# Rebuilding the beginning of a two-block kernel: raw tokens turned once, inverse roots spread by a product, half tiles normed on GpSimd

## The chip, the cores and the metric

The kernel runs on one core of a Trainium2 chip. The metric is the device time of one execution in microseconds (us); several executions are taken and their median is given. The engines are named as the profile names them: PE (TensorE; PEld its weight loads), DVE (VectorE), ACT (ScalarE), POOL (GpSimd) and SP (SyncE, which issues the DMAs).

## The reference

Two transformer blocks over 512 tokens of 1024 channels, in float32. Only the entry of the first block matters here: 16 meta tokens are put ahead of the 512, every row is normed (times the inverse root of its mean square plus 1e-6, times a weight per channel), and the result is multiplied by `w_in`.

```python
h = jnp.concatenate([meta, x], axis=1)      # 16 + 512 tokens, then padding
n = _rms(h, norm_mix_w[l])                  # x * rsqrt(mean(x*x) + eps) * w
z = n @ w_in[l]                             # 1024 -> 9216 channels
q, k, v, glu, g_att, g_conv = jnp.split(z, splits, axis=-1)
...
h = h + m @ w_out[l]                        # the raw h is needed again
```

Attention, a gated convolution, a feed-forward block and a whole second block follow, which the change does not touch.

## The kernel before, in words

Activations are held channel-major: `hT` has 128 channels of a tile on the partitions, 8 tiles (k) and 528 token columns (16 meta + 512). A float32 product is made of three fp32r products: weights and activations are split into a high part and the rest (`wh`, `wl`; `xh`, `xl`), and wh x xh, wh x xl and wl x xh are summed in PSUM. Weights come in chunks of two halves of 128 columns over all 8 k; chunk n uses slot n % 2 of `raw`, `wh` and `wl`. For each chunk ACT makes the high part (`hi(n)`, L1415), DVE the low part (`lo(n)`, L1969), and PE multiplies each half in 8 x 3 x 2 matmuls of 264 columns (`project`, L679).

The order on every engine is written out by hand; each engine runs its own list in order, and semaphores tie the lists together. The beginning before the change:

- SP loads the norm weight row, the meta tokens, four token tiles of 128 tokens each (`xrow`, L537), chunk 0 of the weights in three pieces (k 0-1, 2-3, 4-7, L541), chunk 1, and then some thirty small constants.
- ACT squares each token tile with a row sum (L1442) and takes its root (L1443). DVE inverts the root and scales the tile by it, token-major, into `xn` (L1994).
- PE turns each raw tile (`raw_tokens`, L773, eight transposes of 128x128) for `hT`, and DVE or ACT copies it there (`keep_tokens`, L1998). Separately PE turns the normed tiles, one k at a time over all four token tiles (`normed_tokens`, L780). ACT makes `xh` of that, weighted per channel (L1451), and DVE `xl` (L2007), both from PSUM. The 16 meta columns go through `mn` and `mw` on a path of their own.
- Chunk 0 is multiplied k by k over both token halves (L810), with the transposes of k + 3 behind each k. Then PE turns raw tiles 2 and 3, waits for their copy, and goes on with chunk 1 (`project(ALLP[2], 1, 0, ...)`), whose first half stands ahead of some transposes of constants, and with all later chunks.
- ACT makes the high part of chunk 1 after its token high parts, and DVE `lo(1)` after its token low parts.
- POOL sets constants at the start (L610 to L616) and later copies small attention pieces (L623, L628).

Of the kernel before, what the change touches and what calls it, by code (L numbers as in the profile page):

```python
# [16 lines left out]
D = 1024  # L17
KT = D // 128
# [84 lines left out]
def program(nc, A, out):  # L103
# [17 lines left out]
    with ExitStack() as ctx:  # L121
# [58 lines left out]
        mw = at("mw", [128, KT, NM])  # L180
        xn = at("xn", [128, TT, D])
        mn = at("mn", [NM, D])
# [121 lines left out]
        s_xn = sem("tokens_normed")  # L304
        s_mt = sem("meta_transposed")
        s_mx = sem("meta_weighted")
        s_ms = sem("meta_split")
        s_nt = sem("normed_tokens_transposed")
# [167 lines left out]
        def _(sp):  # L476
# [57 lines left out]
            sp.dma_start(wrow[:], A["norm_mix_w"][0].rearrange("(g p) -> g p", p=128)).then_inc(s_wm, 16)  # L534
            sp.dma_start(mrow[:], A["meta_tokens"]).then_inc(s_min, 16)
            for t in range(TT):
                sp.dma_start(xrow[:, t, :], x[128 * t:128 * (t + 1), :]).then_inc(s_xin[t], 16)  # L537
            G = 3 * D
            for j, (k, signal) in enumerate(zip(PIECES, (s_r0[0], s_r0[1], s_raw[0]))):
# [69 lines left out]
        def _(pool):  # L609
# [6 lines left out]
            pool.memset(eps5[:], 1e-5).then_inc(s_id, 1)  # L616

# [33 lines left out]
        def _(pe):  # L651
# [124 lines left out]
            def normed_tokens(k):  # L776
                if k >= 3:
                    pe.wait_ge(s_nl, k - 2)
                for t in range(TT):
                    ins = tr(scores_ps[:, k % 3, 128 * t:128 * (t + 1)], xn[:, t, 128 * k:128 * (k + 1)], ident[:])  # L780
                ins.then_inc(s_nt, 1)

            pe.wait_ge(s_wm, 16)
            tr(scores_ps[:, 3, 0:8], wrow[:], ident[0:8, 0:8]).then_inc(s_wt, 1)
            pe.wait_ge(s_xin[0], 16)
            raw_tokens(0, psP[0])
            pe.wait_ge(s_min, 16)
            pe.wait_ge(s_xn, 1)
            for k in range(KT):
                tr(scores_ps[:, 3, 128 + NM * k:128 + NM * (k + 1)], mn[:, 128 * k:128 * (k + 1)], ident[0:NM, 0:NM])  # L790
                ins = tr(scores_ps[:, 3, 256 + NM * k:256 + NM * (k + 1)], mrow[:, 128 * k:128 * (k + 1)], ident[0:NM, 0:NM])
            ins.then_inc(s_mt, 1)
            pe.wait_ge(s_xin[1], 16)
            raw_tokens(1, psP[1])
            pe.wait_ge(s_xn, TT + 1)
            for k in range(3):
                normed_tokens(k)
            pe.wait_ge(s_hm, 2)
            pe.wait_ge(s_ms, 2)
            pe.wait_ge(s_l0, 1)  # L800
            for k in range(KT):
                if k == PIECES[1].start:
                    pe.wait_ge(s_l0, 2)
                if k == PIECES[2].start:
                    pe.wait_ge(s_lo, 1)
                pe.wait_ge(s_nl, k + 1)
                for half in range(2):
                    for p, (W, Y) in enumerate(((wh, xh), (wh, xl), (wl, xh))):
                        for a in range(2):
                            ins = mm(psP[half][:, a, 0:HT], W[:, 0, half, k, :], Y[:, k, a * HT:(a + 1) * HT],  # L810
                                     start=(k == 0 and p == 0), stop=(k == KT - 1 and p == 2))
                    if k == KT - 1:
                        ins.then_inc(s_mm, 1)
                if k + 3 < KT:
                    normed_tokens(k + 3)
            for t in range(2, TT):
                pe.wait_ge(s_xin[t], 16)
                raw_tokens(t, psS[t - 2])
# [584 lines left out]
        def _(act):  # L1403
# [31 lines left out]
            act.wait_ge(s_wt, 1)  # L1435
            fn(vmix[:], scores_ps[:, 3, 0:8], ACT.Copy).then_inc(s_wc, 1)
# [3 lines left out]
            for t in range(TT):  # L1440
                act.wait_ge(s_xin[t], 16)
                own(fn(flat, xrow[:, t, :], ACT.Square, accum_out=rcol[:, t:t + 1]))  # L1442
                fn(rcol[:, t:t + 1], rcol[:, t:t + 1], ACT.Sqrt, bias=eps6[:], scale=1.0 / D).then_inc(s_rs, 1)  # L1443
# [5 lines left out]
            def normed_hi(k):  # L1449
                act.wait_ge(s_nt, k + 1)  # L1450
                fn(xh[:, k, NM:T], scores_ps[:, k % 3, :], ACT.Copy, scale=vmix[:, k:k + 1]).then_inc(s_nh, 1)  # L1451

            act.wait_ge(s_mx, 1)
            fn(xh[:, :, 0:NM], mw[:], ACT.Copy).then_inc(s_ms, 1)
            first_hi(0)
            act.wait_ge(s_xt, 2)
            fn(hT[:, :, NM + 128:NM + 256], psP[1][:].rearrange("p a (b c) -> p (a b) c", c=128), ACT.Copy).then_inc(s_hm, 1)
            normed_hi(0)
            normed_hi(1)
            first_hi(1)  # L1460
            normed_hi(2)
            first_hi(2)
            for k in range(3, KT):
                normed_hi(k)
# [497 lines left out]
        def _(dve):  # L1962
# [48 lines left out]
            for t in range(TT):  # L2011
                norm_tokens(t + 1, 128, xrow[:, t, :], xn[:, t, :])
                if t == 0:
                    keep_tokens(0, psP[0])
# [701 lines left out]
```

## Time and profile before

| what | value |
|---|---|
| median of 3 runs | 1545.5 us (1545.24 to 1545.65) |
| the profiled execution | 1544.58 us, span of its instructions 1542.8 us |
| PE busy | 1526.5 us (99%) |
| DVE busy | 1119.0 us (73%) |
| ACT busy | 645.7 us (42%) |
| POOL busy | 29.6 us (2%) |

The profiled execution is a single one, so its time stands beside its span: 1.8 us lie outside of the span. Busy shares are means over the whole span and say little of its first 40 us, which the change touches. Times in the views count from the start of the span.

### The profile page before, as it was taken

What the parts mean: (1) busy time and instruction counts of PE and PEld (TensorE: products, weight loads), DVE (VectorE), ACT (ScalarE), POOL (GpSimd) and SP (SyncE); (2) the same over time, 40 slices, a digit from 0 to 9 for tenths busy, and PEclk for the clock granted to TensorE, in tenths of its full rate; (3) what the DMA queues carried; (4) which work ended last, traced back from release to release, by engine and by line L of the source; (5) the groups of instructions that cost most, each with busy time, mean ns of one, the idle gap of its engine ahead of it and who ended that gap; (6) DMA issues with size and microseconds to landing.
All of it is one profiled execution on the core that took longest, in us unless ns stands there. A gap on an engine that the chain in (4) does not pass through costs nothing.

```text
span 1542.8 us, 25468 instructions
## 1 busy us (share of the span) xinstructions
PE 1526.5 (99%) x9972; PEld 1364.0 (88%) x9972; DVE 1119.0 (73%) x1662; ACT 645.7 (42%) x1014; POOL 29.6 (2%) x66
## 2 busy tenths in 40 slices
PE   8999999999999999999999999999999999999998
PEld 7999999999999999999988888878888888888887
DVE  5889998989665587777764458987748888787123
ACT  5324545545542434434424335744545333333112
POOL 0000010000000000000000020000000000000000
PEclk9999999999999999999999999999999999999999
DMA  6333222232233333233232443231131333332221
GB/s 179 83 92 100 56 69 70 56 83 56 56 89 103 83 101 90 82 103 87 65 94 78 117 110 83 55 82 42 55 110 56 107 92 101 83 107 96 109 82 55
DMA packets 235358, 131.63 MB, mean 85 GB/s; under 512 B 20984, under 2 KB 228740, under 8 KB 235284
## 3 DMA queue, kind: packets, MB, share of 16 engines
q1 hardware_dynamic: 234900, 130.40, 30.1%
q8 instruction: 52, 0.85, 0.2%
q0 software_dynamic: 384, 0.20, 0.1%
q14 instruction: 22, 0.18, 0.0%
HBM read 128.48 MB, written 2.10 MB: 85 GB/s over the span
## 4 chain that ended last, share of the span: by engine, by line
PE 91%; DVE 5%; ACT 3%; issue 1%; DMA 0%; SPq 0%; DVEq 0%; ACTq 0%
PE psP L679 31%; PE psS L679 25%; PE psP L744 8%; PE psS L1363 4%; PE psP L1363 4%; PE psP L701 4%; PE psP L1054 3%; PE psP L1231 1%; DVE conv L2080 1%; PE psS L1231 1%; PE psP L901 1%; DVE wl L1969 1%; PE psS L858 1%; PE psP L810 1%; PE psS L1120 1%
## 5 line engine op out<-in xcount | busy, mean ns | idle before, releaser
L1969 DVE TENSOR_TENSOR wl<-raw,wh 128x2048 fp32r<-128x2048 f32 x124 | 284.0, 2290 | 178.0 <-ACT wh L1415 176.6
L1415 ACT ACTIVATE wh<-raw 128x2048 fp32r<-128x2048 f32 x124 | 237.0, 1912 | 210.0 <-PE psS L1363 74.3
L679 PE MATMUL psP<-xh,wh 128*128 128x258 f32 (+2 forms) x1184 | 295.6, 312 | 1.6 <-ACT mqk L1745 0.6
L679 PE MATMUL psP<-xh,wl 128*128 128x258 f32 (+2 forms) x1184 | 291.6, 309 | 0.0
L679 PE MATMUL psP<-xl,wh 128*128 128x258 f32 (+2 forms) x1184 | 291.4, 309 | 0.0
L679 PE MATMUL psS<-xh,wh 128*128 128x258 f32 (+2 forms) x880 | 209.9, 305 | 0.4 <-DVE hT L1998 0.4
L679 PE MATMUL psS<-xh,wl 128*128 128x258 f32 (+2 forms) x880 | 208.5, 304 | 0.0
L679 PE MATMUL psS<-xl,wh 128*128 128x258 f32 (+2 forms) x880 | 208.1, 303 | 0.0
L679 PEld LDWEIGHTS psP<-xh,wh 128*128 128x128 f32 x1184 | 192.8, 190 | 16.2 <-issue 2.4
L679 PEld LDWEIGHTS psP<-xl,wh 128*128 128x128 f32 x1184 | 192.6, 189 | 12.0 <-issue 0.2
L679 PEld LDWEIGHTS psP<-xh,wl 128*128 128x128 f32 x1184 | 192.4, 189 | 11.9
L2080 DVE SCALAR_TENSOR_TENSOR conv<-u,cdw,conv 128x516 f32<-128x516 f32 x232 | 160.4, 749 | 3.1 <-ACT conv L1483 2.4
L679 PEld LDWEIGHTS psS<-xh,wh 128*128 128x128 f32 x880 | 141.9, 189 | 8.0 <-DVE hT L1998 0.7
L679 PEld LDWEIGHTS psS<-xl,wh 128*128 128x128 f32 x880 | 141.7, 189 | 7.1
L679 PEld LDWEIGHTS psS<-xh,wl 128*128 128x128 f32 x880 | 141.5, 189 | 7.0
L1655 ACT ACTIVATE acth<-prod 128x512 f32 x44 | 27.7, 629 | 196.4 <-DVE prod L2299 196.4
L2293 DVE SCALAR_TENSOR_TENSOR acc<-upr,fdw,acc 128x512 f32<-128x512 f32 x88 | 66.1, 752 | 12.2 <-DVE acc L2292 6.4
L2294 DVE SCALAR_TENSOR_TENSOR acc<-upr,fdw,acc 128x512 f32<-128x512 f32 x88 | 66.2, 752 | 12.1 <-DVE acc L2293 6.4
L744 PE MATMUL psP<-actl,wh 128*128 128x512 f32 x176 | 69.6, 396 | 0.0
L744 PE MATMUL psP<-acth,wl 128*128 128x512 f32 x176 | 69.6, 395 | 0.0
L744 PE MATMUL psP<-acth,wh 128*128 128x512 f32 x176 | 69.6, 395 | 0.0
L2292 DVE TENSOR_SCALAR acc<-upr,fdw 128x512 f32<-128x512 f32 x88 | 48.1, 546 | 17.2 <-DVE upr L2289 16.9
(465 smaller groups left out, 2423.9 us busy)
## 6 DMA issues: line engine op xcount, KB each, us to landing
raw<-in_w_in_dram SPq DMA_DIRECT2D x74, 512.0 KB, 4.9
raw<-in_w_up_dram SPq DMA_DIRECT2D x44, 512.0 KB, 4.9
raw<-in_ffn_up_dram SPq DMA_DIRECT2D x44, 512.0 KB, 5.0
raw<-in_ffn_down_dram SPq DMA_DIRECT2D x22, 512.0 KB, 4.1
raw<-in_w_out_dram SPq DMA_DIRECT2D x16, 512.0 KB, 4.5
raw<-in_w_down_dram SPq DMA_DIRECT2D x16, 384.0 KB, 3.6
raw<-in_w_down_dram SPq DMA_DIRECT2D x16, 320.0 KB, 4.0
raw<-in_w_conv_out_dram SPq DMA_DIRECT2D x8, 512.0 KB, 4.6
```

What stands on the lines that cost most here:

```text
L679: ins = mm(ps[0:rows, a, 0:nn], W[:, s, half, k, 0:rows], Y[:, k, c0 + a * nn:c0 + (a + 1) * nn], start=(k == 0 and p == 0), stop=(k == KT ...
L701: ins = mm(ps[0:r, a, 0:nn], W[:, s, half, k, 0:r], Y[:, k, c0 + a * nn:c0 + (a + 1) * nn], start=(k == 0 and p == 0), stop=(k == KT - 1 a ...
L744: ins = mm(ps[:, 0, :], W[:, k, :], Y[:, kk, :], start=(kk == 0 and p == 0), stop=(kk == FG - 1 and p == 2))
L1054: ins = mm(psP[0][:, half, 256 * a:256 * (a + 1)], Y[:, k, o:o + 128], W[:, n % 2, :, k, :], start=(k == 0 and p == 0), stop=(k == KT - 1 ...
L1231: ins = mm(ZP[t][c], Y[:, k, tok], w, start=(k == 0 and p == 0), stop=(k == KT - 1 and p == 2))
L1363: ins = mm(ALLP[t][:, half, :], Y[:, kk, tok], W[:, j, :], start=(kk == 0 and p == 0), stop=(kk == FG - 1 and p == 2))
L1415: fn(wh[:, n % 2], raw[:, n % 2], ACT.Copy).then_inc(s_hi, 1)
L1969: V.tensor_tensor(wl[:, n % 2], raw[:, n % 2], wh[:, n % 2].bitcast(f32), ALU.subtract).then_inc(s_lo, 1)
L2080: V.scalar_tensor_tensor(y, src, w, y, ALU.mult, ALU.add).then_inc(s_v, 1)
L2292: own(V.tensor_scalar(acc[:, x, :], upr[:, j, x, 4:4 + S], w[2], w[3], ALU.mult, ALU.add))
L2293: own(V.scalar_tensor_tensor(acc[:, x, :], upr[:, j, x, 3:3 + S], w[1], acc[:, x, :], ALU.mult, ALU.add))
L2294: V.scalar_tensor_tensor(acc[:, x, :], upr[:, j, x, 2:2 + S], w[0], acc[:, x, :], ALU.mult, ALU.add).then_inc(s_cva, 1)
```

## The change: what it does

Token-major norming goes. Each raw token tile is turned once, into `hT`. The inverse roots, one per token and token-major, are put on the diagonal of a 128x128 matrix per tile (`diag`), and a product of an all-ones matrix with two such diagonals gives, on all 128 partitions, a row with the inverse roots of 256 tokens. DVE copies it to `rb`. A normed half tile (264 columns of one k) is then `hT` times `rb`: k 0 of the first half is made on DVE, the other fifteen on POOL, into a new `xn`. ACT and DVE make `xh` and `xl` of it, now from SBUF and in half tiles; the meta columns take the same path. PE multiplies chunk 0 by token halves: first all k of columns 0 to 263, then all k of the rest, in the order wh x xh, wl x xh, wh x xl, with the spreading product of the second half behind k 4 of the first. All four raw tiles are turned ahead of chunk 0. Fourteen products of the identity with itself come first on PE. SP loads meta and two token tiles first and mixes weight pieces with the others. The diff, with declarations of semaphores and buffers cut:

```diff
@@ SP @@
+            sp.dma_start(mrow[:], A["meta_tokens"]).then_inc(s_min, 16)
+            tokens(0)
+            tokens(1)
+            sp.dma_start(wrow[:], A["norm_mix_w"][0].rearrange("(g p) -> g p", p=128)).then_inc(s_wm, 16)
+            tokens(2)
+            piece(0, s_r0[0])
+            tokens(3)
+            piece(1, s_r0[1])
+            piece(2, s_raw[0])
             pair(w_in, 1, None, 0, G + 128, G + D + 128)
             inputs()
@@ POOL @@
+            for a in range(2):
+                pool.wait_ge(s_rc, 2 + a)
+                pool.wait_ge(s_hm, 2 * (a + 1))
+                for k in range(1 - a, KT):
+                    if a == 0 and k == 1:
+                        pool.wait_ge(s_xn, 1)
+                    pool.tensor_tensor(xn[:, a, k, :], hT[:, k, a * HT:(a + 1) * HT], rb[:, a * HT:(a + 1) * HT],
+                                       ALU.mult).then_inc(s_xn, 1)
@@ PE @@
-            def normed_tokens(k):
...
+            def spread(t):
+                pe.wait_ge(s_dg, 2 + t // 2)
+                mm(psP[1][:, 1, 128 * t:128 * (t + 2)], ones[:], diag[:, t:t + 2, :].rearrange("p t q -> p (t q)"),
+                   start=True, stop=True).then_inc(s_rb, 1)
+
+            def first_products(a, k):
+                Y = slice(a * HT, (a + 1) * HT)
+                if a == 0 and k == 0:
+                    pe.wait_ge(s_h0, 1)
+                if a == 0 and k == PIECES[1].start:
+                    pe.wait_ge(s_l0, 2)
+                if a == 0 and k == PIECES[2].start:
+                    pe.wait_ge(s_lo, 1)
+                pe.wait_ge((s_fh, s_nh)[a], k + 1)
+                for half in range(2):
+                    mm(psP[half][:, a, 0:HT], wh[:, 0, half, k, :], xh[:, k, Y], start=(k == 0), stop=False)
+                if a == 0 and k == 0:
+                    pe.wait_ge(s_l0, 1)
+                for half in range(2):
+                    mm(psP[half][:, a, 0:HT], wl[:, 0, half, k, :], xh[:, k, Y], start=False, stop=False)
+                pe.wait_ge((s_f0, s_nl)[a], k + 1)
+                for half in range(2):
+                    ins = mm(psP[half][:, a, 0:HT], wh[:, 0, half, k, :], xl[:, k, Y], start=False, stop=(k == KT - 1))
+                    if a == 1 and k == KT - 1:
+                        ins.then_inc(s_mm, 1)
+
+            for _ in range(14):
+                mm(psP[0][:, 0, 0:128], ident[:], ident[:], start=True, stop=True)
+            pe.wait_ge(s_xin[0], 16)
+            raw_tokens(0, psS[0])
...
+            pe.wait_ge(s_xin[1], 16)
+            raw_tokens(1, psS[1])
...
+            pe.wait_ge(s_hm, 1)
+            pe.wait_ge(s_xin[2], 16)
+            raw_tokens(2, psS[0])
+            spread(0)
+            pe.wait_ge(s_hm, 2)
+            pe.wait_ge(s_xin[3], 16)
+            raw_tokens(3, psS[1])
             for k in range(KT):
...
+                first_products(0, k)
+                if k == 4:
+                    spread(2)
             for k in range(KT):
...
+                first_products(1, k)
             pe.wait_ge(s_hm, 3)
             project(ALLP[2], 1, 0, X, 0, HT, None)
@@ ACT @@
+            def token_roots(t):
+                fn(rcol[:, t:t + 2], rcol[:, t:t + 2], ACT.Sqrt, bias=eps6[:], scale=1.0 / D).then_inc(s_rs, 1)
...
+            def normed_hi(a, k):
+                act.wait_ge(s_xn, KT * a + k + 1)
+                fn(xh[:, k, a * HT:(a + 1) * HT], xn[:, a, k, :], ACT.Copy, scale=vmix[:, k:k + 1]).then_inc((s_fh, s_nh)[a], 1)
+
+            token_square(0)
+            token_square(1)
+            token_roots(0)
+            token_square(2)
+            act.wait_ge(s_wt, 1)
+            fn(vmix[:], psP[1][:, 0, 0:8], ACT.Copy).then_inc(s_wc, 1)
             first_hi(0)
+            token_square(3)
+            act.wait_ge(s_wc, 1)
+            normed_hi(0, 0)
+            normed_hi(0, 1)
+            token_roots(2)
             first_hi(1)
+            normed_hi(0, 2)
+            normed_hi(0, 3)
             first_hi(2)
+            for k in range(4, KT):
+                normed_hi(0, k)
+            for k in range(KT):
+                normed_hi(1, k)
@@ DVE @@
+            def diagonals(t):
+                dve.wait_ge(s_rs, 2 + t // 2)
+                own(V.reciprocal(rcol[:, t:t + 2], rcol[:, t:t + 2]))
+                for j in range(t, t + 2):
+                    ins = V.tensor_scalar(diag[:, j, :], ident[:], rcol[:, j:j + 1], None, ALU.mult)
+                ins.then_inc(s_dg, 1)
+
+            def copy_roots(t):
+                dve.wait_ge(s_rb, 2 + t // 2)
+                V.tensor_copy(rb[:, NM + 128 * t:NM + 128 * (t + 2)], psP[1][:, 1, 128 * t:128 * (t + 2)]).then_inc(s_rc, 1)
...
+            def first_normed_lo(a, k):
+                dve.wait_ge((s_fh, s_nh)[a], k + 1)
+                Y = slice(a * HT, (a + 1) * HT)
+                V.scalar_tensor_tensor(xl[:, k, Y], xn[:, a, k, :], vmix[:, k:k + 1], xh[:, k, Y].bitcast(f32),
+                                       ALU.mult, ALU.subtract).then_inc((s_f0, s_nl)[a], 1)
...
+            keep_tokens(1, psS[1])
+            diagonals(0)
+            copy_roots(0)
+            dve.wait_ge(s_hm, 2)
+            dve.wait_ge(s_rc, 2)
+            V.tensor_tensor(xn[:, 0, 0, :], hT[:, 0, 0:HT], rb[:, 0:HT], ALU.mult).then_inc(s_xn, 1)
             first_lo(0)
+            dve.wait_ge(s_wc, 1)
+            first_normed_lo(0, 0)
+            first_normed_lo(0, 1)
+            keep_tokens(2, psS[0])
             first_lo(1)
+            first_normed_lo(0, 2)
+            diagonals(2)
+            first_normed_lo(0, 3)
             first_lo(2)
+            first_normed_lo(0, 4)
+            copy_roots(2)
+            keep_tokens(3, psS[1])
+            for k in range(5, KT):
+                first_normed_lo(0, k)
+            for k in range(KT):
+                first_normed_lo(1, k)
...
             lo(1)
-            for t in range(2, TT):
-                keep_tokens(t, psS[t - 2])
```

## Rows read from the trace of the kernel before

**Rows 1.** The page, chain of work that ended last: share of the span by engine.

```profile
PE 91%; DVE 5%; ACT 3%; issue 1%; DMA 0%; SPq 0%; DVEq 0%; ACTq 0%
```

**Rows 2.** That chain in the first 100 us: start us, us, what, xcount.

```profile
2.53 5.88 DMA xrow<-in_x_dram
...
12.32 2.82 PE psS L780 x12
15.14 1.81 PE psP L810 x12
...
29.39 0.89 PE psS L773 x8
...
30.30 1.24 DVE hT L1998
...
31.57 6.11 PE psS L679 x48
...
44.65 11.68 PE psP L679 x96
```

**Rows 3.** Tile view of `xrow`: duration ns min/median/max, first and last start us.

```profile
L773 PE MATMUL psP<-ident,xrow x16: 421/421/475, 5.4 to 10.7; 128*128 128x128 f32 x16
...
L773 PE MATMUL psS<-ident,xrow x16: 271/272/273, 29.2 to 30.9; 128*128 128x128 f32 x16
```

**Rows 4.** Timeline of the beginning, all engines: start us, us, engine line op.

```profile
0.75 0.41 SPq L534 DMA_DIRECT2D wrow<-in_norm_mix_w_dram  x1
...
5.44 1.97 PE L773 MATMUL psP<-ident,xrow 128*128 128x128 f32 x8 [2.90 <-DMA xrow<-in_x_dram]
...
9.15 1.97 PE L773 MATMUL psP<-ident,xrow 128*128 128x128 f32 x8
...
9.78 0.28 DVE L2019 COPY hT<-psS 128x128 f32<-128x128 f32 x1
...
12.38 0.69 DVE L2003 TENSOR_TENSOR wl<-raw,wh 128x512 fp32r<-128x512 f32 x1
...
17.09 1.23 DVE L2003 TENSOR_TENSOR wl<-raw,wh 128x1024 fp32r<-128x1024 f32 x1
...
25.62 1.91 ACT L1415 ACTIVATE wh<-raw 128x2048 fp32r<-128x2048 f32 x1
...
27.56 2.29 DVE L1969 TENSOR_TENSOR wl<-raw,wh 128x2048 fp32r<-128x2048 f32 x1 [1.05 <-ACT wh L1415]
```

**Rows 5.** Timeline of DVE in the second block, operations of 256 columns.

```profile
1159.19 0.48 DVE L2635 SCALAR_TENSOR_TENSOR xl<-hT,vec,xh 128x256 fp32r<-128x256 f32 x1
1159.59 0.48 DVE L2629 SCALAR_TENSOR_TENSOR hT<-psP,vec,hT 128x256 f32<-128x256 f32 x1
```

**Rows 6.** Groups by line, 1100 to 1250 us: xcount | busy us, mean ns | idle before.

```profile
L1921 ACT ACTIVATE xh<-hT,vec 128x256 fp32r<-128x256 f32 x16 | 8.0, 507 | 2.3 <-DVE hT L2629 2.2
```

**Rows 7.** Timeline of PE: four float32 products with the all-ones matrix.

```profile
411.83 1.03 PE L757 MATMUL psP<-sacc,ones 128*128 128x258 f32 x4
```

**Rows 8.** Timeline of POOL: two copies of attention values, one select.

```profile
163.12 1.93 POOL L623 COPY vr<-qkv 128x64 f32<-128x64 f32 x1 [0.49 <-ACT qkv L1514]
...
194.77 2.17 POOL L623 COPY vr<-qkv 128x64 f32<-128x64 f32 x1
...
915.59 2.66 POOL L635 TENSOR_SCALAR_AFFINE_SELECT sel<-sel 4x512 f32<-4x512 f32 x1
```

**Rows 9.** Timeline of DVE at the same three places.

```profile
162.67 2.29 DVE L1969 TENSOR_TENSOR wl<-raw,wh 128x2048 fp32r<-128x2048 f32 x1 [0.16 <-ACT wh L1415]
...
194.56 2.29 DVE L1969 TENSOR_TENSOR wl<-raw,wh 128x2048 fp32r<-128x2048 f32 x1
...
915.49 2.28 DVE L1969 TENSOR_TENSOR wl<-raw,wh 128x2048 fp32r<-128x2048 f32 x1
```

**Rows 10.** Groups of POOL by line: xcount | busy us, mean ns | idle before.

```profile
L631 POOL MEMSET wab<- 128x768 f32 x1 | 0.7, 739 | 520.1 <-PE psS L757 520.1
...
L638 POOL TENSOR_SCALAR_AFFINE_SELECT tri<-tri 128x128 f32<-128x128 f32 x1 | 0.3, 283 | 0.0
```

More of the change, by code:

```diff
@@ L533, in _, with tokens, piece @@
             x = A["x"][0]
-            sp.dma_start(wrow[:], A["norm_mix_w"][0].rearrange("(g p) -> g p", p=128)).then_inc(s_wm, 16)
-            sp.dma_start(mrow[:], A["meta_tokens"]).then_inc(s_min, 16)
-            for t in range(TT):
+            G = 3 * D
+            def tokens(t):
                 sp.dma_start(xrow[:, t, :], x[128 * t:128 * (t + 1), :]).then_inc(s_xin[t], 16)
-            G = 3 * D
-            for j, (k, signal) in enumerate(zip(PIECES, (s_r0[0], s_r0[1], s_raw[0]))):
+            def piece(j, signal):
+                k = PIECES[j]
                 for half in range(2):
                     sp.dma_start(raw[:, 0, half, k], kp(w_in)[:, k, G + D * half:G + D * half + 128]).then_inc(signal, 16)
+            sp.dma_start(mrow[:], A["meta_tokens"]).then_inc(s_min, 16)
[7 more added lines that the diff above has]
+            piece(2, s_raw[0])
             pair(w_in, 1, None, 0, G + 128, G + D + 128)
@@ L798, in _ @@
-            pe.wait_ge(s_hm, 2)
-            pe.wait_ge(s_ms, 2)
-            pe.wait_ge(s_l0, 1)
-            for k in range(KT):
[L802 to L815, printed above, removed]
@@ new lines, in _ @@
+            for _ in range(14):
+                mm(psP[0][:, 0, 0:128], ident[:], ident[:], start=True, stop=True)
+            pe.wait_ge(s_xin[0], 16)
+            raw_tokens(0, psS[0])
+            pe.wait_ge(s_min, 16)
+            for k in range(KT):
+                ins = tr(psP[0][:, 1, 128 + NM * k:128 + NM * (k + 1)], mrow[:, 128 * k:128 * (k + 1)], ident[0:NM, 0:NM])
+            ins.then_inc(s_mt, 1)
+            pe.wait_ge(s_dg, 1)
+            mm(psP[0][:, 1, 0:NM], ones[0:NM, :], diag[0:NM, TT, 0:NM], start=True, stop=True).then_inc(s_rb, 1)
@@ new lines, in _ @@
+            own(V.reciprocal(rcol[0:NM, TT:TT + 1], rcol[0:NM, TT:TT + 1]))
+            V.tensor_scalar(diag[0:NM, TT, 0:NM], ident[0:NM, 0:NM], rcol[0:NM, TT:TT + 1], None, ALU.mult).then_inc(s_dg, 1)
+            keep_tokens(0, psS[0])
+            dve.wait_ge(s_mt, 1)
+            dve.wait_ge(s_rb, 1)
+            V.tensor_copy(hT[:, :, 0:NM], psP[0][:, 1, 128:128 + KT * NM].rearrange("p (k c) -> p k c", c=NM))
+            V.tensor_copy(rb[:, 0:NM], psP[0][:, 1, 0:NM]).then_inc(s_rc, 1)
+            keep_tokens(1, psS[1])
@@ L2029, in _ @@
+            diagonals(2)
+            first_normed_lo(0, 3)
             first_lo(2)
-            for k in range(3, KT):
-                first_normed_lo(k)
+            first_normed_lo(0, 4)
[3 more added lines that the diff above has]
+                first_normed_lo(0, k)
+            for k in range(KT):
+                first_normed_lo(1, k)
             def constants():
@@ L2044, in _ @@
             lo(1)
-            for t in range(2, TT):
-                keep_tokens(t, psS[t - 2])
+            dve.wait_ge(s_f0, KT)
+            dve.wait_ge(s_nl, KT)
             V.memset(u[:, :, 0:PAD], 0.0)
```

81 lines of the change are left out of this document (12 added, 69 removed).

## The prediction, as it was made before the run

> **What bounds the kernel now.** I read the chain of work that ended last first. TensorE holds 91% of it [rows 1], so the edited beginning matters only by when TensorE's unbroken run starts. The chain inside the first 100 us shows that moment [rows 2]: it passes from token tile 2's landing (2.53 + 5.88 = 8.41) through roots and norms to the normed transposes at 12.32, the first chunk's products at 15.14, the two late raw tiles at 29.39 and the copy at 30.30, and at 31.57 chunk 1's first half begins. From there on TensorE runs without a hole, 11.68 us a chunk. So the question is when that half chunk can begin after the change; call it S, 31.57 now. What follows S is the same instructions in the same order, and I count a shift of S in full at the end.
>
> Next I read the tile view of `xrow` [rows 3]: a transpose takes 421 ns at the start and 272 ns later. I read these as the 1.2 and the 2.4 GHz level: TensorE's clock rises only at about 15 us here. Then the timeline of the beginning, for durations [rows 4].
>
> **The change, first stretch: to the first half tile.** Meta and token loads move ahead of the weight row, whose issue takes 0.41 us; token tile 0, on which TensorE starts at 5.44, should land near 4.95 [rows 4]. Fourteen products on the identity come first, from about 1.7 us; at the lower level eight transposes of the same 128 columns take 1.97 us, so these end by about 4.8 and delay nothing. Then, on TensorE, eight transposes (1.97, ends 6.95), eight small meta transposes instead of sixteen (those filled 7.41 to 9.15, so 0.6 with the clock up, 1 without) and one small product, 0.25, to 7.8. Token tile 1: 1.1 us at the upper level, 1.97 at the lower. I take the upper from here, since TensorE has then worked from 1.7 us on; to 8.95. VectorE copies the tile (1.24, as at 30.30 [rows 2]) to 10.2; a reciprocal and two 128-column diagonals, no row of their shape, lie between nothing and two 128-column copies (0.28 each [rows 4]) and a reciprocal: 0.4, to 10.6. The spreading product has 256 columns: four such with 258 took 1.03 us together [rows 7], so one alone, with start and tail, lies between a quarter of that and the whole; I take 0.48, to 11.1. The copy of 256 columns from PSUM lies between 0.28 (128) and 1.24 (1024), 0.42 on their line; to 11.6. The first product on VectorE, 264 columns, 0.43 on the line through 0.69 (512) and 1.23 (1024) [rows 4]; to 12.06. ScalarE's high part of it, 0.51 [rows 6], to 12.6. First matmul at 12.7, against 15.14: the head gains 2.4 us.
>
> **Second stretch: the first half's queue on VectorE.** The new order puts between that product and the low part of tile (0, 4): three weight low parts (0.60, 0.60, 1.15 without their overlapped tails), a raw tile copy (1.14), root work (0.45) and five low parts of 264 columns. Two such of 256 start 0.39 to 0.40 us apart [rows 5], so 1.98 for five. Sum 5.92, tail 0.08: 6.0 us. At the same time GpSimd makes its seven products. Here the trace has something to say. GpSimd's 64-column copies at 163.12 and 194.77 took 1.93 and 2.17 us and ended at 165.05 and 196.94, each 0.09 us after VectorE's weight low part, which reads two SBUF tensors (162.67 + 2.29 = 164.96; 194.56 + 2.29 = 196.85) [rows 8, 9]. So GpSimd doesn't read beside such an operation. All VectorE's low parts here are of that kind. Whether VectorE is held in turn by a long GpSimd instruction no row shows, since those copies are too short: held not at all is one end, for the whole instruction the other. I take the second, because the first is already exclusive.
>
> What a GpSimd product of two 264-column inputs takes has no row either. The select on 512 columns ended at 918.25, 0.48 us after VectorE's low part (915.49 + 2.28 = 917.77) had let it go [rows 8, 9]; as the copies need less than 0.09 us past such an end, I give it 0.57. The 128-column one took 0.283, and a memset writes 768 columns in 0.739, 0.96 ns each [rows 10]. The line through the two selects gives 0.38 for one input of 264; that is the lower end, a second input free. Doubled, 0.76 is the upper. A second input as one more pass, somewhat under the memset's rate, at 0.83 ns a column, makes 0.38 + 0.22 = 0.60, which I take.
>
> With seven products of 0.60 (4.2 us) beside these 6.0 us, about half falls under the raw copy from PSUM or under VectorE's waits for ScalarE; I charge VectorE 2.1 us. Low part (0, 4) is ready at 12.06 + 6.0 + 2.1 = 20.2.
>
> **Third stretch: what the second half waits for.** The spreading product of the second half stands on TensorE behind the products of tile 4, so behind that low part: 0.3 for the last two matmuls, 0.48 product, 0.42 copy, then raw tile 3's copy, 1.24: 22.6. Only then may GpSimd begin its eight products; it first lets one low part pass, 0.3. One turn is a product and a low part, less the overlaps seen above (0.09 at a GpSimd start; 0.48 lasts, 0.40 apart): 0.60 - 0.09 + 0.48 - 0.08 = 0.91, say 0.88 with ScalarE's time between hidden. Last product at 22.9 + 7 x 0.88 + 0.60 = 29.7. TensorE's six matmuls a tile (0.73 from 0.122 each, 11.68 / 96 [rows 2]) fit under the turn. What is late next is chunk 1's weight: its high part is queued on ScalarE behind all sixteen token high parts, its low part on VectorE behind all sixteen low ones, and chunk 1 waits for it. So 0.46 for the last high part, then 1.91 and 2.29 [rows 4], with 0.1 for hops: S = 34.45. Before, this pair ran at 25.62 and 27.56, ended at 29.85 and cost nothing, covered by the rest of chunk 0; that cover of 1.7 us is gone.
>
> 34.45 - 31.57 = +2.9 us. The removed work (32 normed transposes, 2.82 us for the first twelve, and the two late raw tiles) is in this: TensorE alone could be through chunk 0 at 12.7 + 96 x 0.122 + 0.48 = 24.9, against 29.39, and the elementwise chain gives that back. SP's queue keeps its bytes. Tile 0 and tile 2 landed 3.0 us apart, 1.5 us for 512 KB, so in the new order the weight pieces land near 8.9, 11.1 and 13.0; ScalarE comes to them at 9.3, 13.9 and 15.4 and they cost nothing, each late microsecond of the first would cost one. The constants' loads keep their place and have until S + 6 us. Chunk 2's weight load waits for the third weight low part, 19.8, and stands behind the constants' loads anyway.
>
> On the profiled execution's own 1544.58 us (span 1542.8) this makes 1547.5; the runs' median lies 0.9 above that execution, so 1548.4.
>
> **A rule weighed.** The rows show GpSimd held by VectorE [rows 8, 9]. The Trainium skill (SBUF — State Buffer, section "SBUF: two separate sides") says more: the pair of ports that the two engines share is an exclusive lock, taken for a whole instruction by whichever starts first, and a VectorE operation with two SBUF inputs is locked out by a GpSimd one that reads SBUF. By that rule the sum stands as made; the trace agrees in the one direction that it shows. The Trainium skill (GPSIMD Engine Reference, section "3.1 Elementwise — side-by-side cycle accounting") gives 4497 ns for a two-input product of 2048 columns, by proportion 0.58 us for 264 columns, an estimate; the sum by it would be about 0.3 us lower, and no run here shows it yet.
>
> **The rivals.**
> GpSimd waits but holds nobody, or the two share freely. For: no row shows VectorE held. Against free sharing: GpSimd does wait [rows 8, 9]. Then a turn is 0.60 to 0.75, VectorE's 2.1 us fall away in part or whole, and S comes to between 30.0 (free) and 32.4 (GpSimd alone waits): 1543.9 to 1546.3. With a free second input (0.38) as well, 2.9 us are gained, 1542.6; nothing in the order lets it go further, since the chain of stretches two and three remains.
>
> The GpSimd product costs more than I take: the other side. Place: the eight products of the second half and the seven of the first. Price: 0.1 us more on each adds about 1.45 us, so 0.76 gives +5.2, 1550.7. It decides from about 0.62 us a product, where S is 3.1 us late and the loss passes 0.2%. For it: two-input work on GpSimd has no row. Against it: the select's 0.283.
>
> The clock doesn't come up. The identity products are to raise it before the tokens; if it stays at 1.2 GHz until about 13 us, tile 1 and the spreading product cost 2.0 us more on the path: 1550.4. For: in the trace TensorE worked from 5.44 to 11.1 with small holes and was still at the lower level at 12.32, twelve transposes in 2.82 us [rows 2 to 4]. Against: there are 3 us of extra work ahead now.
>
> **How the numbers follow.** 0.2% of this kernel, 3.1 us, is about what a measurement can tell from no change. My case (both held, product near 0.60, 1547 to 1549.2) gets 0.37, a fifth of it beyond 1548.6; the sharing rival 0.31, nearly all within 0.2%; the costlier product 0.19, the late clock 0.07, both slower; 0.06 is left for something that I don't see and that gains over 3.1 us. So faster 0.06, slower 0.19 + 0.07 + 0.08 and some for the sharing rival with a late clock, 0.37, same 0.57. The range runs from the lower sharing case, 1543.6, to the costlier product just beyond its bound, 1551.5.
>
> **What would show it.** In the changed trace: first matmul of the chunk near 12.7; GpSimd's products longer than 0.7 us where a low part is under way, and low parts longer than 0.48; the second spreading product after 20 us; the eight GpSimd products of the second half from about 23; high and low part of chunk 1's weight after 29.7 and directly ahead of S. It is wrong if S stands below 30, if TensorE alone sets the end of chunk 0, or if GpSimd's products come at steps over 1.1 us.

## The result, and the profile after

The changed kernel takes 1551.4 us (median of 6 runs, 1550.62 to 1553.62) against 1545.4 for the kernel before beside it (1544.76 to 1546.49): ratio 1.0042, 95% interval 1.0032 to 1.0052. It is slower by 0.4%. I had forecast 1548.4, 2.9 us later, and "no change" as likeliest; the loss is about twice that. The time lies just inside the range, and that is luck: the range ended where it did because of the costlier product, which is not what cost the time.

The chain's shares first, the line that answers to [rows 1]. POOL, which had no part in the chain, now has 1% of it:

```profile
PE 90%; DVE 6%; ACT 3%; issue 1%; POOL 1%; DVEq 0%; POOLq 0%; ACTq 0%
```

The chain in the first 100 us (start us, us, what), which answers to [rows 2]:

```profile
1.68 5.42 PE psP L824 x28
...
12.99 0.45 DVE xn L2069
...
21.58 0.81 PE psP L812 x2
22.39 0.44 PE psP L816 x2
22.83 0.44 PE psP L819 x2
23.27 0.87 PE psP L799 x2
...
24.58 1.14 DVE hT L2043
...
25.86 7.19 POOL xn L636 x8
...
33.49 1.91 ACT wh L1446
...
35.43 2.30 DVE wl L2009
...
37.87 6.08 PE psS L700 x48
...
50.91 11.68 PE psP L700 x96
```

Chunk 1 begins at S = 37.87 in place of 31.57, and from there the steps are the old ones: 6.08 us for its first half (before 6.11), 11.68 a chunk. The spans, 1549.1 and 1542.8, differ by the same 6.3 us. So all of the loss lies ahead of S. The chain names it: 28 records of identity products, a stretch at 21.6 in which a pair of matmuls takes 0.44 us, eight POOL products one behind the other, then the weight of chunk 1, high part and low part.

Windows of the changed kernel: start and end, length, busy us (instructions) of PE, PEld, DVE, ACT and POOL, then the granted TensorE clock, DMA share, GB/s.

```profile
13.00:31.50 18.50, 13.73 (x69) 11.79 (x68) 15.82 (x23) 8.37 (x17) 11.94 (x14) 0.72 0.48 122
...
18.00:20.00 2.00, 1.48 (x10) 1.05 (x9) 1.96 (x5) 1.43 (x4) 1.90 (x3) 0.91 0.29 88
20.00:22.00 2.00, 1.23 (x4) 0.92 (x5) 1.93 (x3) 0.45 (x1) 0.00 (x0) 0.50 0.29 72
...
28.00:30.00 2.00, 2.00 (x12) 2.00 (x10) 2.00 (x3) 1.20 (x3) 2.00 (x3) 0.53 0.59 151
30.00:32.00 2.00, 2.00 (x19) 2.00 (x18) 2.00 (x3) 1.03 (x2) 2.00 (x3) 1.00 0.00 0
```

The first of these windows in the kernel before:

```profile
13.00:31.50 18.50, 18.13 (x143) 17.57 (x141) 11.21 (x14) 10.56 (x13) 0.00 (x0) 1.00 0.51 133
```

Before, PE worked 18.1 of these 18.5 us at the upper level. Now it works 13.7, part of it at the lower level (0.50 of full speed, 1.2 GHz, from 19.6 to 29.9), while DVE went from 11.2 to 15.8 us. The limit has moved from PE to DVE and POOL.

The tile views of `xl`, `xn` and `diag` (duration ns min/median/max) show why both are so full:

```profile
L2053 DVE SCALAR_TENSOR_TENSOR xl<-xn,vmix,xh x16: 479/974/993, 14.2 to 33.7; 128x264 fp32r<-128x264 f32 x16
...
L636 POOL TENSOR_TENSOR xn<-hT,rb x15: 741/938/1202, 13.6 to 32.1; 128x264 f32<-128x264 f32 x15
...
L2034 DVE TENSOR_SCALAR diag<-ident,rcol x4: 281/436/780, 11.2 to 19.2; 128x128 f32<-128x128 f32 x4
```

A low part takes 0.48 us when POOL is idle and mostly 0.97 when it isn't; a product takes 0.74 beside a copy from PSUM and 0.94 beside a low part. The diagonals are held too, though they read only one tile and a single column from SBUF: the two of the first half, with POOL idle, took 0.28 us each, the two of the second half, at 18.70 and 19.21, 0.59 and 0.78, and each ended 0.08 us after the product that was under way.

### The profile page after: what moved, and what is told of

Its sections match the earlier page's. It is cut to its first block, busy times and chain, and to the rows that moved or that the text cites. A ratio compares the mean times of both kernels' runs of the same rounds, so it can differ in the third digit from the quotient of the medians.

```text
span 1549.1 us, 25491 instructions
## 1 busy us (share of the span) xinstructions
PE 1530.1 (99%) x9966; PEld 1366.2 (88%) x9966; DVE 1125.4 (73%) x1671; ACT 646.9 (42%) x1018; POOL 43.2 (3%) x81
## 4 chain that ended last, share of the span: by engine, by line
PE 90%; DVE 6%; ACT 3%; issue 1%; POOL 1%; DVEq 0%; POOLq 0%; ACTq 0%
PE psP L700 31%; PE psS L700 25%; PE psP L765 8%; PE psS L1394 4%; PE psP L1394 4%; PE psP L722 4%; PE psP L1085 3%; PE psP L1262 1%; DVE conv L2135 1%; PE psS L1262 1%; PE psP L932 1%; DVE wl L2009 1%; PE psS L889 1%; PE psS L1151 1%; ACT wh L1446 1%
```

## The experiments

All changes are to the changed kernel unless something else is said. In all twelve kernels below and the two already shown, the span less S is 1511.1 to 1511.4 us, with three exceptions that are named where they occur; so S is the measure, and the ratios of whole runs, with intervals of about 0.1% to each side, say less. But S comes from one execution of each kernel, and not from the median one. In the nine kernels that open with fourteen identity products as the changed one does, VectorE's first product began between 12.86 and 13.84 us (12.99 in the changed kernel), so a difference in S of less than 1 us has to be read beside that.

**Terms of the head: the identity products.**

```diff
-            for _ in range(14):
+            for _ in range(7):
                 mm(psP[0][:, 0, 0:128], ident[:], ident[:], start=True, stop=True)
```

> Seven identity products in place of fourteen. Theory (each is two passes, 0.43 us at 1.2 GHz, so fourteen end at 7.1 and hold token tile 0 back by 2 us): seven end near 4.7, tile 0 is turned from 5.0 on, the first normed half tile is ready 1.0-1.6 us earlier than 13.4 and chunk 1 starts as much earlier, 36.3-36.9, about 1550.2 us. Rival (the fourteen earn their cost, because with seven the clock rises later): first half tile at 13.2 or later, 1551.2 us or above.

Measured 1550.13 us, ratio 1.0029 (1.0018 to 1.004). Its chain:

```profile
12.05 0.44 DVE xn L2069
...
24.91 7.21 POOL xn L636 x8
...
36.93 7.60 PE psS L700 x48
```

VectorE's first product starts at 12.05, 0.94 us earlier than the changed kernel's 12.99 and 0.81 earlier than the earliest with fourteen, and S is 36.93, 0.94 earlier too: both just short of what the theory set, and far from the rival. The products beyond the seventh did delay the head. But the first half of chunk 1 takes 7.60 us in place of 6.08: TensorE's clock fell here, 0.6 us into it. That gives 1.5 us back (span less S 1512.8) in this execution, at 1551.89 us the slowest of the eight.

**The lower clock from 20.4 us.** Eleven identity products more, at places where TensorE waits in the first half:

```diff
             def first_products(a, k):
                 Y = slice(a * HT, (a + 1) * HT)
+                if a == 0 and k in (2, 3, 4):
+                    for _ in range(5 if k == 2 else 3):
+                        mm(psP[0][:, 1, 0:128], ident[:], ident[:], start=True, stop=True)
```

> Adds eleven products of the identity with itself on TensorE inside the first half, ahead of its waits at tiles 2, 3 and 4. Theory (TensorE's clock falls to 1.2 GHz near 20.4 us and that delays the spreading product of the second half): the matmuls keep 0.28 us and 0.12 steps from 15 to 35 us, the second spreading product ends near 23 instead of 24.13, chunk 1 starts at 36.4-36.8, about 1550.1 us. Rival (the clock costs nothing here, since VectorE and GpSimd set the pace): chunk 1 starts at 37.9 or later by what the added products cost, 1551.4 us or above.

Measured 1551.89 us, ratio 1.0043 (1.0027 to 1.006): no gain. Chain and windows:

```profile
24.85 7.20 POOL xn L636 x8
...
36.86 7.63 PE psS L700 x48
```

```profile
24.00:26.00 2.00, 0.84 (x6) 0.78 (x6) 2.00 (x4) 0.25 (x1) 1.15 (x2) 1.00 0.17 38
...
37.00:41.00 4.00, 4.00 (x21) 4.00 (x22) 2.23 (x13) 0.00 (x0) 0.00 (x0) 0.59 0.72 212
```

The clock stayed up through 26 us (it was at the lower level from 26.7 to 30.1), the second half's POOL products began 1.0 us earlier, and S came to 36.86, 1.0 us earlier, just beyond the theory's late end; the theory's time was missed. For the clock fell again as chunk 1 began, at 36.9, and its first half took 1.55 us more (span less S 1512.8). The idle time ahead of S was 2.14 us here, 2.50 with seven products and 2.26 in the changed kernel, where the clock did not fall; what decides this I can't tell from these runs.

**The queue of chunk 1's weight.** High and low part moved ahead of the second half's pieces, to where VectorE stood idle from 21.9 to 24.1:

```diff
@@ ACT @@
+            hi(1)
             for k in range(KT):
                 normed_hi(1, k)
@@ DVE @@
             first_normed_lo(0, 4)
+            lo(1)
             copy_roots(2)
...
-            lo(1)
```

> High and low part of chunk 1's weight move ahead: high part on ScalarE behind the first half's token high parts, low part on VectorE behind token low part (0, 4), where VectorE is idle from 21.9 to 24.2. Theory (chunk 1 waits for its own weight split, queued last): the copy of the second half's roots comes 0.4 us later, chunk 1 starts right at the end of chunk 0's matmuls, near 36.1 instead of 37.87, about 1549.6 us. Rival (the low part of 2.29 us only changes its place in a chain of GpSimd and VectorE that is as long as before): chunk 1 at 37.5 or later, 1551 us.

Measured 1549.39 us, ratio 1.0028 (1.0018 to 1.0037), S 35.86: 2.0 us of the 6.3 come back, a quarter of a microsecond more than was expected. The tail behind the last low part, 4.8 us in the changed kernel, is gone, but VectorE's 2.29 us now delay tile 3's copy (24.98 against 24.50) and the clock is at the lower level while TensorE works off what has piled up.

**The late spread.** Spreading product, diagonals and copies of the second half moved forward:

```diff
@@ DVE @@
             first_normed_lo(0, 1)
+            diagonals(2)
             keep_tokens(2, psS[0])
             first_lo(1)
             first_normed_lo(0, 2)
-            diagonals(2)
+            copy_roots(2)
             first_normed_lo(0, 3)
+            keep_tokens(3, psS[1])
             first_lo(2)
             first_normed_lo(0, 4)
-            copy_roots(2)
-            keep_tokens(3, psS[1])
@@ PE @@
-                if k == 4:
+                if k == 1:
                     spread(2)
```

> The second half's roots are spread earlier: on TensorE behind the products of tile 1 instead of tile 4, and on VectorE its diagonals, the copy of the roots and raw tile 3's copy stand two to four operations further ahead. Nothing is left out. Theory (the third stretch: the late spread sets when GpSimd begins its eight products, 25.86 us in the changed kernel, and VectorE stands still from 21.9 to 24.1 for it): GpSimd begins at 21.5 to 22.5, VectorE has no hole left and becomes the limit, S (first product of chunk 1, 37.87 in the changed kernel) 34.3 to 35.5. Rival (VectorE's queue only changes its order): S at 37.0 or later.

Measured 1548.42 us, ratio 1.0022 (1.0012 to 1.0031). The chain:

```profile
21.99 7.93 POOL xn L636 x8
...
30.37 1.91 ACT wh L1446
...
32.31 2.31 DVE wl L2009
...
34.75 6.09 PE psS L700 x48
```

POOL begins at 21.99 in place of 25.86 and S is 34.75, as the theory had it: 3.1 us of the 6.3. This place, the third stretch of the prediction, is the largest single one that was tried.

**Both orders together.** The edit above, and `hi(1)` and `lo(1)` between the halves:

```diff
                 first_normed_lo(0, k)
+            lo(1)
             for k in range(KT):
                 first_normed_lo(1, k)
```

> The early spread of the run before, and chunk 1's weight split ahead of the second half's pieces (high part on ScalarE behind the eighth high part, low part on VectorE behind the eighth low part). Nothing is left out. Theory (VectorE is the limit once the holes are gone, so moving the split moves none of its work): S 34.0 to 35.5, within 0.7 us of the run before, slower than before the change by 2.5 to 4 us. Rival (the order and the waits were the whole cause): S at 32.0 or earlier, the time of the kernel before or better.

Measured 1549.89 us, ratio 1.0034 (1.002 to 1.0049), S 35.98: worse than the early spread alone by 1.2 us. Neither bound was met. The tile views show what I had missed:

```profile
L636 POOL TENSOR_TENSOR xn<-hT,rb x15: 735/937/2806, 13.5 to 30.7; 128x264 f32<-128x264 f32 x15
...
L2011 DVE TENSOR_TENSOR wl<-raw,wh x1: 2839/2839/2839, 26.4 to 26.4; 128x2048 fp32r<-128x2048 f32 x1
```

The weight's low part, 2.29 us elsewhere, waited 0.55 us for a product and then held the next product for the whole of its time (2.81 us). No low part came to TensorE from 26.4 to 30.1, it worked 1.84 of the 4 us from 28, and then nearly the whole second half was still to go.

**The mutual holding, taken away.** A low part reads PSUM in place of `xn`, so that it has one input tile in SBUF; its values are then other data. First this is done in the second half of the changed kernel (the edit below), then in that of the one with both orders, then, with the early spread alone, in all low parts from tile 4 of the first half on (`if a or k >= 4`).

```diff
-                V.scalar_tensor_tensor(xl[:, k, Y], xn[:, a, k, :], vmix[:, k:k + 1], xh[:, k, Y].bitcast(f32),
+                V.scalar_tensor_tensor(xl[:, k, Y], psS[0][:, 0, 0:HT] if a else xn[:, a, k, :], vmix[:, k:k + 1], xh[:, k, Y].bitcast(f32),
```

> The eight token low parts of the second half read a PSUM bank in place of xn (their values are other data), so each has one SBUF input left; all counts and sizes stay. Theory (GpSimd's products and VectorE's two-input low parts hold each other): the eight GpSimd products, 0.94 us each at steps of 0.90 in the changed kernel, fall to 0.60-0.65 at steps of 0.55-0.65, the low parts from 0.98 to 0.48 us, and chunk 1 starts about 2.3 us earlier, at 35.6 instead of 37.87: about 1549.1 us. Rival (a GpSimd product of 264 columns takes 0.9 us by itself): products and steps stay at 0.9, start of chunk 1 at 37.9, 1551.4 us.

> As the run before, but the eight low parts of the second half read the first PSUM tile in place of the normed half tile, so that they have one input in SBUF and not two; their values are other data (this part of the computation is changed). Theory (what is left of the loss is the mutual holding of VectorE and GpSimd): these low parts take 0.49 us in place of 0.97, VectorE's work shrinks by some 3.5 us, and S comes to 30.5 to 32.3, no later than before the change. Rival (the holding costs only where one of the two would have waited anyway): S within 1 us of the run before.

> The early spread (S 34.75 there) with the low parts of the first half's tiles 4 to 7 and of the whole second half reading the first PSUM tile in place of the normed half tile; their values are other data (this part of the computation is changed). Theory (a low part with both inputs in SBUF and a GpSimd product hold each other): those five that overlap a product take 0.49 us in place of 0.97, GpSimd's steps are 0.71 in place of 0.90, the last high part is some 1.3 us earlier, and S comes to 33.0 to 33.9. Rival (the holding hides behind other waits): S at 34.4 or later.

In the changed kernel: 1550.52 us, ratio 1.0035 (1.0023 to 1.0048), S 37.32, between the two bounds and nearer the rival's. The eight products took 6.24 us in place of 7.19: three were still held by low parts of the first half (0.86 to 0.94 us), the other five took 0.75 to 0.76 at steps of 0.71, where the theory had 0.60 to 0.65. The head happened to be 0.4 us later. The rival's 0.9 us for a product by itself is refuted all the same. With both orders: 1549.03 us, ratio 1.0026 (1.0016 to 1.0035), S 35.31, the rival's side: there TensorE is the limit after 30 us, and a faster VectorE helps little. With the early spread: 1547.05 us, ratio 1.0012 (1.0003 to 1.0022), S 33.71 against 34.75, as the theory had it. Its tile views:

```profile
L636 POOL TENSOR_TENSOR xn<-hT,rb x15: 740/751/1593, 13.8 to 28.0; 128x264 f32<-128x264 f32 x15
...
L2053 DVE SCALAR_TENSOR_TENSOR xl<-psS,vmix,xh x12: 477/486/494, 23.1 to 29.4; 128x264 fp32r<-128x264 f32 x12
```

The same two kinds of work at the same time: 0.49 in place of 0.97 for the low part, 0.75 in place of 0.94 for the product, and all that was changed is where one input lies. (The longest, 1.593, ran beside a weight's low part.) The holding needs GpSimd at work as well: in the last kernel below, where it does nothing, all sixteen low parts read two tiles from SBUF and take 0.49.

**What GpSimd takes off VectorE.** With the early spread, all fifteen products on VectorE, each ahead of the low part of the tile before:

```diff
@@ DVE @@
+            def product(a, k):
+                V.tensor_tensor(xn[:, a, k, :], hT[:, k, a * HT:(a + 1) * HT], rb[:, a * HT:(a + 1) * HT], ALU.mult).then_inc(s_xn, 1)
...
+                if k + 1 < KT:
+                    product(1, k + 1)
                 first_normed_lo(1, k)
```

> The early spread with all fifteen GpSimd products moved to VectorE, each one place ahead of the low part of the tile before it; GpSimd does nothing here. Nothing is left out. Theory (the holding is nearly exclusive, so GpSimd takes nothing off VectorE): VectorE gets 6 us more of products of its own, and its last low part still ends between 31.0 and 32.5, against 31.82 with GpSimd; chunk 1's weight, whose high part now comes later, ends S at 35.0 to 36.2. Rival (GpSimd's products take work off VectorE, as they were meant to): the last low part ends at 36 or later, S at 39.

Measured 1548.42 us, ratio 1.0022 (1.0012 to 1.0031): the same as with GpSimd. The start and the end of the chain, and the view of `diag`:

```profile
1.69 6.26 PE psP L824 x28
...
30.27 0.36 DVE xn L2070
...
31.07 1.91 ACT wh L1446
...
33.00 2.30 DVE wl L2009
...
35.44 7.45 PE psS L700 x48
```

```profile
L2034 DVE TENSOR_SCALAR diag<-ident,rcol x4: 281/284/287, 12.0 to 16.7; 128x128 f32<-128x128 f32 x4
```

VectorE's last low part ends at 31.7 (31.198 + 0.494), with GpSimd at 31.8. Beside a VectorE that reads two SBUF inputs, GpSimd's fifteen products relieved it of nothing. They even cost it something: the identity products took 6.26 us in this execution, 5.40 in the one with GpSimd, so VectorE began 0.86 us later here (first product at 13.84 and 12.98), and counted from there its queue took 17.9 us without GpSimd and 18.8 with it. All four diagonals take 0.28 here. (The first half of chunk 1 is again partly at the lower clock, 7.45 us, after 3.12 us without work, so the span less S is 1512.6; this execution, 1549.83 us, is the slowest of the ten.)

**The kernel before with identity products.**

```diff
+            for _ in range(14):
+                mm(psP[0][:, 0, 0:128], ident[:], ident[:], start=True, stop=True)
             pe.wait_ge(s_wm, 16)
             tr(scores_ps[:, 3, 0:8], wrow[:], ident[0:8, 0:8]).then_inc(s_wt, 1)
```

> The kernel before, with the fourteen identity products ahead of its first transpose and nothing else. Theory (the clock alone is worth what the identity products are for): raw tile 0 is turned about 2 us later, the clock is at its upper level by 12.3, the twelve normed transposes take 1.3 to 1.6 us in place of 2.82, S 30.0 to 30.4 in place of 31.57, 1.2 to 1.6 us less than before. Rival (the clock falls again in the holes before 12.3, or the late raw tile holds the head): S at 31.3 or later.

Measured 1548.46 us, ratio 1.0019 (1.0009 to 1.0028): slower, S 35.95. The chain:

```profile
1.69 5.97 PE psP L784 x28
...
7.92 0.18 ACT vmix L1438
8.10 1.04 ACT sq L1440 x2
...
15.97 2.82 PE psS L780 x12
18.79 2.58 PE psP L812 x12
```

I had looked at TensorE's queue alone. The weight row is turned behind the identity products, ScalarE waits for it before its squares (8.10, where the kernel before made the meta tokens' square at 3.29), and the twelve normed transposes, the reason for the whole thing, come at 15.97 and again at the lower level. So the run does not say what the clock alone would be worth there.

**The idea without its costs.** VectorE makes the normed tokens straight from the PSUM tile of the raw turn, 1024 columns at a time; ScalarE copies the raw tiles; GpSimd has no part; seven identity products; the second run puts the queues in another order.

```diff
@@ DVE @@
+                V.tensor_tensor(xn[:, :, c0:c0 + n_], src, rb[:, c0:c0 + n_].rearrange("p (o c) -> p o c", o=1).to_broadcast([128, KT, n_]),
+                                ALU.mult).then_inc(s_xn, 1)
...
+                norm(psS[t % 2][:].rearrange("p a (b c) -> p (a b) c", c=128), NM + 128 * t, 128)
@@ ACT, second run @@
             first_hi(2)
             normed_hi(0, 4)
             normed_hi(0, 5)
+            keep_tokens(1)
             normed_hi(0, 6)
             normed_hi(0, 7)
+            hi(1)
+            keep_tokens(2)
             for k in range(KT):
                 normed_hi(1, k)
+            keep_tokens(3)
```

> The idea of the change without what it cost: tokens turned once and raw, the roots spread by a product, but VectorE makes the normed tokens straight from the PSUM tile, 1024 columns at a time (four operations of some 1.25 us in place of sixteen of 264 columns), the copies of the raw tiles go to ScalarE, GpSimd does nothing here, seven identity products in place of fourteen, the first roots spread ahead of token tile 1, chunk 1's weight split between the second half's pieces. Nothing is left out. Theory (the loss was the place of the normed products, the queue behind them and the late spread, not the single raw turn itself): first matmul of the chunk at 12.5 to 13.5, S 27.0 to 29.5, faster than before the change by 2 to 4.5 us. Rival (ScalarE or VectorE is as full as it was): S at 31 or later.

> The run before with its queues put in another order, nothing left out: the weight row is turned ahead of the roots' product, VectorE norms tile 0 before ScalarE copies it, the copies of raw tiles 1 to 3 stand where ScalarE would wait, the second half's roots are taken ahead of the first low part, chunk 1's high part comes between the two halves on ScalarE and its low part last on VectorE. Theory (what held the run before was its order, above all the split of chunk 1's weight ahead of five low parts, 28.2 to 30.4 us, which left TensorE idle and let its clock fall): chunk 0's products start at 13.5 to 14.5, TensorE keeps its upper level from 24 us on, S 27.5 to 29.5, time 2 to 4 us less than before the change. Rival (the two queues are too full in any order): S at 31.5 or later.

The first: 1548.66 us, ratio 1.0021 (1.0012 to 1.003), S 35.75, first matmul at 14.84. The theory failed on both numbers. Its chain has `lo(1)` at 28.29 ahead of five low parts, TensorE idle for 1.6 us behind it, and then the lower clock:

```profile
28.29 2.20 DVE wl L2028
30.49 0.41 DVE xl L2072
...
30.95 0.55 PE psP L819 x2
31.50 0.44 PE psP L812 x2
```

The second: 1542.64 us (1542.15 to 1543.56, 11 runs) against 1545.22, ratio 0.9984 (0.9975 to 0.9993). It beats both kernels. S is 30.31, 0.8 later than I had expected it at the latest (the first matmul of the chunk is at 14.77); by the spans, 1541.5 and 1542.8, it gains 1.3 us, by the medians 2.6. Windows and the view of `xn`:

```profile
16.00:20.00 4.00, 3.92 (x23) 3.52 (x23) 2.99 (x6) 4.00 (x8) 0.00 (x0) 1.00 0.15 42
20.00:24.00 4.00, 3.90 (x32) 3.69 (x32) 3.72 (x6) 2.92 (x3) 0.00 (x0) 1.00 0.27 61
```

```profile
L2068 DVE SCALAR_TENSOR_TENSOR xl<-xn,vmix,xh x16: 485/491/496, 14.8 to 27.2; 128x264 fp32r<-128x264 f32 x16
L2080 DVE TENSOR_TENSOR xn<-psS,rb x4: 1217/1224/1225, 10.5 to 22.5; 128x1024 f32<-128x1024 f32 x4
```

Four operations of 1.22 us do the work of the sixteen products (a small fifth one norms the meta columns), and all low parts take 0.49. From about 18 us on TensorE is nearly always busy and at the upper level; before that the clock column says 1.00, but the matmuls come at steps of 0.22 us, those of the lower level. This kernel differs from the changed one in several places at once, so it shows that the idea can gain, by 0.16%, and not what each place is worth.

## Why the prediction was wrong, by its own steps

S was to be 34.45 and is 37.87, 3.42 us later; the time was to be 1548.4 and is 1551.4. The mechanism that I took, two engines that hold each other and chunk 1's weight queued last, is what happens. What failed is the price of the identity products in the first stretch and the clock that the third stretch took for granted; the other terms were off by less.

- **First stretch, 1.38 us short** (first product's end 13.44, predicted 12.06; first matmul of the chunk 14.20, predicted 12.7). This is the step that failed first: I priced an identity product like a transpose, some 0.22 us at the lower level. The trace has 28 records for 14 products, two to a product, about 0.43 us a product at that level, and they end at 7.11 in place of 4.8. They did not "delay nothing", since tile 0 had to wait for them. Of these 2.3 us about 1.0 is left behind tile 0, because its eight transposes then ran at the upper level, 0.87 us in place of 1.97, and seven products fewer bring 0.94 back. The spreading product has two records as well (0.71 for 0.48), and the root work ahead of it took 0.6 for 0.4. The x4 in [rows 7], too, are records: I read four products, and the kernel makes two there.
- **Second stretch, 0.35 short** (from that end to the low part (0, 4): 8.49, predicted 8.14). The 2.1 us charged for holding on VectorE were about right in sum: its operations took some 1.8 us longer than alone. But 0.8 of that fell on the two diagonals, which I had not seen as operations that can be held.
- **Third stretch, 1.39 short** (to tile 3's copy: 3.79, predicted 2.4). The order was as I had it, the second spread behind tile 4 and POOL behind that; but TensorE's clock had fallen to the lower level at 19.6 (its first matmul after that came at 20.4). So the first pair of tile 4 ran until 0.46 us after that low part, and the four matmuls left and the spread took 1.75 us (22.39 to 24.13) in place of 0.78. Extra work in the holes brings 1.0 back. I had a rival in which the clock doesn't come up, none in which it comes up and falls again; the change itself makes the holes, by taking transposes out of TensorE's queue and making it wait for VectorE.
- **POOL's eight products, 0.26 short.** Step 0.89, predicted 0.88; from tile 3's copy to the last one's end 7.32, predicted 7.06. The product by itself was mis-sized: 0.74 beside a copy from PSUM, where I took 0.60. When it waits for a low part, it ends 0.60 us after that one (25.855 + 0.857 = 26.712; the low part ended at 26.113), so some 0.14 us of it seem to pass beside the other, and the turn came out right. The rival of the costlier product was thus half true, and harmless here.
- **The tail, right**: from the last product's end to S 4.83, predicted 4.79. High part 1.91, low part 2.30, both uncovered.

The terms add up: 1.38 + 0.35 + 1.39 + 0.26 + 0.04 = 3.42. What the whole change lost, 6.3 us, is not the sum of what single edits bring back (0.94, 1.0, 2.0 and 3.1), since they share the same waits. The early spread with the weight ahead lost ground against the early spread alone, because a weight's low part in that place starves TensorE. The rival that "the two share freely" is refuted by the durations, 0.97 against 0.49 and 0.94 against 0.75. Nor was its S of 30.0 near: with most of the holding taken away and the spread early, S was still 33.71.

The rule that I weighed held. The Trainium skill (SBUF — State Buffer, "SBUF: two separate sides") has the shared ports held for a whole instruction by whoever starts first. The trace agrees in both directions: 0.97 against 0.49 for the low part, and 2.81 us for a product behind a weight's low part of 2.29 us that had itself waited. The other figure, 4497 ns, the Trainium skill (GPSIMD Engine Reference, "3.1 Elementwise — side-by-side cycle accounting") gives for a two-input operation, there an addition, of 2048 columns. The estimate from it by proportion, 0.58 us for 264 columns, lies near the 0.60 measured behind a low part and under the 0.74 measured free.

## What to carry to other kernels

Before work is moved off the busiest engine, add up the queues of those that take it, in the window that counts: between 13 and 31.5 us VectorE was busy 4.6 us more than before and TensorE 4.4 us less, because it waited. Work on GpSimd left VectorE undisturbed here only beside operations that take a tile from PSUM: the copies (1.21 us with and without it) and the low parts that read one (0.49). Beside GpSimd's products the low parts with two tiles in SBUF went from 0.48 to 0.97, and the diagonals, with one, from 0.28 to 0.59 and 0.78. The kernel that gained norms in larger operations straight from PSUM and leaves GpSimd out. When TensorE is no longer the limit, its holes can cost a second time through the clock, so work that is late should come ahead of filler, and a long operation on VectorE must not stand between TensorE and its next pieces.

## What the runs showed of the hardware that I had not expected

- A plain float32 product has two records, of 213 ns a step for 128 columns at the lower level; a float32 transpose of the same shape has one.
- The moment at which TensorE comes to its upper level varies from run to run: the same 28 records took 5.29 to 6.26 us in the nine kernels with the same head (in the longest every step from the second on is 0.213 us, in the others the last steps are 0.112). The clock column says 1.00 there; the lower level of the beginning is read from the steps alone. The fall at 19.6 us in the changed kernel does show in the column, after 0.65 us of work in the 2 us from 16 and 1.48 in those from 18.
- Ending earlier can be worth nothing: with waits ahead of S of 2.14 and 2.50 us the clock fell and chunk 1's first half took 7.6 us, with 2.26 us it did not and took 6.08. Why is open.
- A VectorE operation with a single input tile in SBUF, the diagonal, took 0.59 and 0.78 us beside GpSimd products and 0.28 without, so a second input tile is not needed for an operation to be held. The low part with its other tile in PSUM has one in SBUF as well and was not held; what sets the two apart no run shows.
- The weight's low part on VectorE took 2.84 us behind a GpSimd product, and a GpSimd product 2.81 us behind that.
